# Two attention blocks whose value projection is computed by tokens and ahead of attention

## The chip, the cores and the metric

The program runs on one core of a Trainium2 chip. The metric is the device time of one execution in microseconds; lower is better. The engines named below are TensorE (PE in the profile), VectorE (DVE), ScalarE (ACT), GpSimd (POOL) and SyncE (SP, which here issues nearly all DMAs). Each runs its own instruction stream in order and waits on semaphores that the others raise.

## The reference

Two transformer stacks of two layers run one after the other on 512 tokens with 1024 features, all in float32. The change touches the input projections of the first stack's two attention mixers:

```python
# layer 0, hybrid mixer: n is the RMS-normed input (512 x 1024)
proj = n @ w_in                      # 3 x 512 (dilated) + 3 x 512 (forgetting) + 8 forget gates
qa, ka, va, qb, kb, vb, fb = split(proj)
oa = dilated_attention(rope(qa) * s, rope(ka), va)
ob = forgetting_attention(qb * s, kb, vb, cumsum(log_sigmoid(fb + b_f)))
h  = h + concat(oa, ob) @ w_out
# layer 1, differential mixer
q, k, v = split(n @ w_qkv)           # 3 x 1024; rope on all of q and k
o  = (softmax(q1 k1^T) - lam * softmax(q2 k2^T)) @ v       # 8 heads, v 128 wide
h  = h + subln(o) @ w_out
```

A gated feed-forward block follows each mixer; the second stack (gated linear attention, latent attention, convolutions) is untouched.

## The kernel before

**Weights and precision.** All large products go by "weight tiles": 128 output features by 1024 input features (512 KB), 25 of them in the hybrid projection (8 q, 8 k, 8 v, one for the forget gate) and 24 in the differential one. SP loads a tile into `raw`, ACT rounds it to `whi` (`split_hi`, L656), POOL subtracts to get `wlo` (`split_lo`, L566; from tile 14 of the differential projection on DVE does it, `split_lo_dve`, L573), and PE multiplies in `gemm` (L685 to L687): for each of 8 slices of 128 input features three matmuls, `whi` with `n_hi`, `whi` with `n_lo`, `wlo` with `n_hi`, 24 matmuls of 512 columns a tile, into one of two `G` banks. There are two slots for tiles, so the split of tile n+2 waits for the product of tile n.

**The norm's factor.** `n_hi` and `n_lo` hold the input times the gain, not yet divided by its root mean square. `norm_sum` on PE adds the squares (two float32 matmuls into bank S), ACT makes `rstd` from the sum by Ln and Exp (`rms_scale_act`, L775 and L776), and DVE multiplies each product by `rstd` as it takes it out of PSUM (`take_scaled`, L672). In the hybrid block the sum stands behind half of the second tile, in the differential block behind half of the first.

**Tiles, ahead of attention and in it.** q and k tiles leave the product with features on partitions, as attention wants them. A value tile must have tokens on partitions, so DVE takes it to `vst`, PE transposes it in four 128x128 blocks into bank X (`transpose_pe`, L1300), and DVE copies it to `v` (`keep_v_dve`, L1315). Four tiles (q0, k0, q1, k1) come ahead of attention; the others follow in its steps, 6 of the 8 slices of a tile in each step, in the order v0 q2 k2 v1 q3 k3 and so on. After a q or k tile SP turns its halves by four DMAs (L530) and DVE ropes it in three operations (L1322 to L1324), in the hybrid block for heads 0 to 3 only.

**Attention steps.** Each block has 32 units (8 heads or pairs of heads by 4 blocks of queries, the longest first: 512, 384, 256 and 128 keys), and 37 steps. In step s PE makes the scores of unit s, with every fourth step the value products (L1839 and L2071) of a head that is through, then the transposes of the probabilities of unit s-2, then the projection's slices of this step, and in the differential block every fourth step the head's norm sum (L2092). DVE takes the scores out with mask and maximum (L1968, L2200), scales the probabilities of the unit before, and then does what the tiles ask; ACT does the exponentials, copies the transposes to `pt`, and splits the next tile. The scores of unit s+1 wait until both halves of unit s are taken out of bank S (`masked`). When the input tiles are used up, the eight tiles of the first half of the output projection follow at one in a step (12 matmuls each), and two more begin in the last steps.

## Time and profile before

| | |
|---|---|
| device time, three runs | 2508.21, 2508.33, 2510.48 us (median 2508.33) |
| span of the profiled execution | 2506.5 us |
| PE busy | 2457.9 us (98%) |
| DVE, ACT, POOL busy | 1567.8 (63%), 1038.5 (41%), 975.0 (39%) |
| mean granted TensorE clock | 0.998 |
| hybrid attention, first to last scores | 34.59 to 225.48 us |
| differential attention, first to last scores | 649.61 to 836.87 us |

For the profiled execution the profile gives the span from first to last instruction; the device times come from runs of their own, 1.8 us above it at the median. Busy shares are averages over all stages; what a change in a stage is worth is read from that stage's waits. A matmul record of 0.39 us is the passage of one matmul; in a stream of them one starts every 0.227 us.

### The profile page before, as it was taken

Reading aid. Unit: us, or ns where it says so; the run is one execution under the profiler, and the core shown is the slowest. Engines: PE = TensorE matmul, PEld = TensorE weight load, DVE = VectorE, ACT = ScalarE, POOL = GpSimd, SP = SyncE. Lnnn points to the kernel's source line nnn. Section 1 sums busy time; section 2 is a strip of 40 time slices with the busy share of each in tenths; the row PEclk is TensorE's granted clock in tenths of the full one; section 3 lists DMA queues with packets and bytes.
Section 4 is the critical chain, followed back from the end, with each engine's and each line's share of the span. In section 5 each row is a group of like instructions: output and inputs, shape, how many; then the busy total and the mean of one; then the engine's idle time right before and its main releaser. Section 6 shows DMA issues by size and latency. Waiting matters only on the chain.

```text
span 2506.5 us, 33281 instructions
## 1 busy us (share of the span) xinstructions
PE 2457.9 (98%) x11238; PEld 1900.1 (76%) x11238; DVE 1567.8 (63%) x2255; ACT 1038.5 (41%) x1574; POOL 975.0 (39%) x421
## 2 busy tenths in 40 slices
PE   9999999999999999999999999999999999999998
PEld 6777788888777688888777467888877746788886
DVE  7654663777677766177778657515557875751555
ACT  5444552332344554123463654313336365431333
POOL 2232444444310045444455034444455504443443
PEclk9999999999999999999999999999999999999999
DMA  5222323232322233223222022323322202222232
GB/s 178 88 82 66 97 92 105 92 103 94 101 86 79 64 101 101 91 92 105 80 88 71 14 70 82 104 88 101 105 80 88 76 13 72 84 102 91 92 105 80
DMA packets 66510, 219.59 MB, mean 88 GB/s; under 512 B 8552, under 2 KB 8808, under 8 KB 66288
## 3 DMA queue, kind: packets, MB, share of 16 engines
q1 hardware_dynamic: 64384, 214.79, 26.2%
q10 hardware_dynamic: 2032, 3.56, 0.4%
q8 instruction: 58, 0.95, 0.2%
q14 instruction: 36, 0.29, 0.0%
HBM read 209.91 MB, written 2.11 MB: 85 GB/s over the span
## 4 chain that ended last, share of the span: by engine, by line
PE 86%; DVE 6%; ACT 3%; issue 3%; POOL 1%; DMA 0%; SPq 0%; DVEq 0%; POOLq 0%; ACTq 0%
PE bank_G L685 25%; PE bank_G L687 25%; PE bank_G L686 25%; PE bank_X L2435 1%; PE bank_S L1825 1%; PE bank_X L1853 1%; PE bank_O L2071 1%; PE bank_O L1839 1%; PE bank_S L2060 1%; PE bank_S L1612 1%; PE bank_S L2339 1%; PE bank_O L1622 1%; PE bank_O L2536 1%; PE bank_X L2083 0%; PE bank_X L2524 0%
## 5 line engine op out<-in xcount | busy, mean ns | idle before, releaser
L566 POOL TENSOR_TENSOR wlo<-raw,whi 128x1024 fp32r<-128x1024 f32 (+2 forms) x361 | 884.4, 2451 | 1478.7 <-ACT whi L656 1423.4
L685 PE MATMUL bank_G<-n_hi,whi 128*128 128x512 f32 x2216 | 881.8, 398 | 7.9 <-POOL wlo L566 3.2
L687 PE MATMUL bank_G<-n_hi,wlo 128*128 128x512 f32 x2216 | 864.1, 390 | 0.0
L686 PE MATMUL bank_G<-n_lo,whi 128*128 128x512 f32 x2216 | 863.3, 390 | 0.0
L656 ACT ACTIVATE whi<-raw 128x1024 fp32r<-128x1024 f32 (+2 forms) x389 | 404.3, 1041 | 676.0 <-PE bank_G L687 675.4
L685 PEld LDWEIGHTS bank_G<-n_hi,whi 128*128 128x128 f32 x2216 | 416.5, 188 | 110.3 <-issue 13.2
L687 PEld LDWEIGHTS bank_G<-n_hi,wlo 128*128 128x128 f32 x2216 | 416.1, 188 | 88.2
L686 PEld LDWEIGHTS bank_G<-n_lo,whi 128*128 128x128 f32 x2216 | 416.6, 188 | 86.8 <-issue 4.3
L685 PE MATMUL bank_G<-a_hi,whi 128*128 128x512 f32 x704 | 275.2, 391 | 0.0
L686 PE MATMUL bank_G<-a_lo,whi 128*128 128x512 f32 x704 | 274.1, 389 | 0.0
L687 PE MATMUL bank_G<-a_hi,wlo 128*128 128x512 f32 x704 | 274.0, 389 | 0.0
L2001 DVE TENSOR_TENSOR h<-h,bank_G 128x512 f32<-128x512 f32 x88 | 60.3, 686 | 158.2 <-PE bank_G L687 158.2
L686 PEld LDWEIGHTS bank_G<-a_lo,whi 128*128 128x128 f32 x704 | 132.2, 188 | 28.2 <-issue 0.7
L685 PEld LDWEIGHTS bank_G<-a_hi,whi 128*128 128x128 f32 x704 | 132.2, 188 | 28.0 <-issue 0.7
L687 PEld LDWEIGHTS bank_G<-a_hi,wlo 128*128 128x128 f32 x704 | 132.2, 188 | 27.3
L1145 ACT ACTIVATE a_hi<-prod 128x512 f32 (+1 forms) x88 | 55.7, 633 | 232.7 <-DVE prod L1209 232.7
L1209 DVE TENSOR_TENSOR prod<-silu,up 128x512 f32<-128x512 f32 x44 | 86.8, 1973 | 64.3 <-ACT silu L1152 64.3
L1211 DVE TENSOR_TENSOR a_lo<-prod,a_hi 128x512 f32 (+1 forms) x88 | 64.0, 727 | 80.1 <-ACT a_hi L1145 80.1
L1094 DVE SCALAR_TENSOR_TENSOR h<-h,bank_G 128x512 f32 x24 | 16.5, 687 | 144.8 <-PE bank_G L687 144.8
L1202 DVE TENSOR_SCALAR conv_up<-bank_G,vec 128x512 f32<-128x512 f32 x42 | 31.5, 750 | 110.3 <-PE bank_G L687 110.3
L2883 DVE SCALAR_TENSOR_TENSOR bank_O<-cpad,vec,bank_O 128x512 f32<-128x512 f32 x116 | 78.3, 748 | 3.8 <-DVE decayed L2390 2.8
L1195 DVE SCALAR_TENSOR_TENSOR conv<-gate,vec,conv 128x512 f32<-128x512 f32 x46 | 68.6, 1492 | 7.1 <-DVE conv L1194 7.0
(358 smaller groups left out, 2859.7 us busy)
## 6 DMA issues: line engine op xcount, KB each, us to landing
raw<-in_w_mix_in SPq DMA_DIRECT2D x40, 512.0 KB, 3.3
raw<-in_w_hyb_in SPq DMA_DIRECT2D x25, 512.0 KB, 3.3
raw<-in_w_diff_in SPq DMA_DIRECT2D x24, 512.0 KB, 3.3
raw<-in_w_up0a SPq DMA_DIRECT2D x22, 512.0 KB, 3.3
raw<-in_w_up0b SPq DMA_DIRECT2D x22, 512.0 KB, 3.2
raw<-in_w_up1a SPq DMA_DIRECT2D x22, 512.0 KB, 3.2
raw<-in_w_up1b SPq DMA_DIRECT2D x22, 512.0 KB, 3.2
raw<-in_w_up2a SPq DMA_DIRECT2D x22, 512.0 KB, 3.3
```

Source lines behind the costliest of these rows:

```text
L566: pool.tensor_tensor(b.wlo[:, g.slot, w], b.raw[:, g.slot, w], b.whi[:, g.slot, w], ALU.subtract).then_inc(b.lo_ready, 1)
L656: act.activation(b.whi[:, g.slot, w], b.raw[:, g.slot, w], ACT.Copy).then_inc(b.hi_ready, 1)
L685: pe.matmul(out, b.whi[:, g.slot, w], hi[:, hi_at + k, :], start=(k == 0), stop=False)
L686: pe.matmul(out, b.whi[:, g.slot, w], lo[:, lo_at + k, :], start=False, stop=False)
L687: mm = pe.matmul(out, b.wlo[:, g.slot, w], hi[:, hi_at + k, :], start=False, stop=(k == pieces - 1))
L1145: act.activation(b.a_hi[:, j, :], b.prod[:, :], ACT.Copy).then_inc(b.act_hi, 1)
L1195: return dve.scalar_tensor_tensor(dst[:, :], src[:, s + 2:s + 2 + T], v_(b, w, 2 * FC + c), dst[:, :], ALU.mult, ALU.add)
L1202: link(dve.tensor_scalar(dst[:, :], src, v_(b, w, FC + c), None, ALU.mult))
L1209: dve.tensor_tensor(b.prod[:, :], b.silu[:, :], up, ALU.mult).then_inc(b.prod_done, 1)
L1211: dve.tensor_tensor(b.a_lo[:, at, :].rearrange("p a t -> p (a t)"), b.prod[:, :], b.a_hi[:, at, :].rearrange("p a t -> p (a t)"), ALU.subt ...
L2001: dve.tensor_tensor(h, h, b.G[:, g.slot, :], ALU.add).then_inc(b.evacuated, 1)
L2883: dve.scalar_tensor_tensor(b.O[:, j, :], b.cpad[:, j, bass.ds(i + (first + 1), T)], v_(b, f"cfm_dw{l}", 2 * i + (2 * first + 2 + j)), b.O[ ...
```

## The change

Both projections are rearranged in the same way.

- **Value tiles.** A value tile is now 256 input features by 512 output features (the host rearranges the weights). The normed input is the stationary side and the weights move: for each slice of 128 input features and each of the four blocks of 128 tokens, three matmuls of 512 columns. Four tiles fill four PSUM banks with half of the value matrix, tokens on partitions; eight tiles make all of it. A tile still has 24 matmuls. The first half goes to X0, X1, O0, O1, the second to S1, S0, X0, X1.
- **The factor.** It is now one number per partition. `norm_sum` stands behind the second value tile in both blocks; behind the third, four small matmuls turn `rstd` into a column per token block in G, DVE copies it (`keep_column_dve`), and ACT takes the eight banks out with that scale (`keep_values_act`). Taking to `vst`, the transposes and the copies to `v` are gone.
- **Order.** The eight value tiles come first, then q0, k0, q1, k1: twelve tiles ahead of attention. The others (and the forget gate, thirteenth in the hybrid block) follow in attention, 4 slices, half a tile, in each step, q and k in turn. SP's turning DMAs in the opening of the program go with the q and k tiles to their later place.

```diff
--- before.py
+++ after.py
 POST_HYB = 0
-POST_DIFF = POST_HYB + 8 + 64
-POST_NORM = POST_DIFF + 8 + 32
+POST_DIFF = POST_HYB + 64
+POST_NORM = POST_DIFF + 32
 POST_MIX = POST_NORM + 8
...
-    gemm(pe, b, Index(a.g0), b.n_hi, b.n_lo, KD, lambda k: pe.wait_ge(b.nlo_ready, k + 1))
-    gemm(pe, b, Index(a.g0 + 1), b.n_hi, b.n_lo, KD, None, range(KD // 2))
-    pe.wait_ge(b.square_in, 16)
-    norm_sum(pe, b, 0)
-    gemm(pe, b, Index(a.g0 + 1), b.n_hi, b.n_lo, KD, None, range(KD // 2, KD))
+    value_tiles_pe(pe, b, a, 0, 0)
...
-    first_gemms_n(pe, b, ATT_DIFF.g0, 24, 2)
+    value_tiles_pe(pe, b, ATT_DIFF, 24, 2)
     inputs_start_pe(pe, b, ATT_DIFF)
 
 
 def hyb_in_act(act, b):
     for n in range(1, ATT_HYB.lead):
+        if n in VALUE_ENDS:
+            keep_values_act(act, b, ATT_HYB, VALUE_ENDS.index(n))
         split_hi(act, b, Index(ATT_HYB.g0 + n + 2))
 
 
 def diff_in_act(act, b):
     for n in range(ATT_DIFF.lead):
+        if n in VALUE_ENDS:
+            keep_values_act(act, b, ATT_DIFF, VALUE_ENDS.index(n))
         split_hi(act, b, Index(ATT_DIFF.g0 + n + 2))
...
-def input_follow_pe(pe, b, a, n):
-
-    kind, o = a.tiles[n]
-    if kind == "v":
-        transpose_pe(pe, b, Index(a.g0 + n), Index(a.in_posts[n]), b.vst[:, o % 2, :])
+VALUE_TILES, VALUE_ENDS = 8, (3, 7)
+VALUE_COLUMNS = 4 * P
+def value_bank(b, group, j):
+    return ((b.X, 0), (b.X, 1), (b.O, 0), (b.O, 1))[j] if group == 0 else ((b.S, 1), (b.S, 0), (b.X, 0), (b.X, 1))[j]
+def value_tile_pe(pe, b, a, n, nlo):
+    g, (group, t) = Index(a.g0 + n), divmod(n, 4)
+    pe.wait_ge(b.lo_ready, g.n + 1)
+    for s in range(2):
+        k, w = 2 * t + s, slice(s * VALUE_COLUMNS, (s + 1) * VALUE_COLUMNS)
+        pe.wait_ge(b.nlo_ready, nlo + k + 1)
+        for j in range(NB):
+            x, slot = value_bank(b, group, j)
+            if group == 1 and k == 0 and j >= 2:
+                pe.wait_ge(b.v_kept, VALUE_TILES * a.n + j - 1)
+            out, rows = x[:, slot, :], slice(j * P, (j + 1) * P)
+            pe.matmul(out, b.n_hi[:, k, rows], b.whi[:, g.slot, w], start=(k == 0), stop=False)
+            pe.matmul(out, b.n_lo[:, k, rows], b.whi[:, g.slot, w], start=False, stop=False)
+            mm = pe.matmul(out, b.n_hi[:, k, rows], b.wlo[:, g.slot, w], start=False, stop=(k == KD - 1))
+            if k == KD - 1 and j < NB - 1:
+                mm.then_inc(b.v_done, 1)
+    mm.then_inc(b.gemm_done, 1)
+def value_tiles_pe(pe, b, a, nlo, q):
+    for n in range(VALUE_TILES):
+        value_tile_pe(pe, b, a, n, nlo)
+        if n == SUM_BEHIND[a.n]:
+            pe.wait_ge(b.square_in, 16)
+            norm_sum(pe, b, q)
+        if n == 2:
+            pe.wait_ge(b.rstd_ready, q + 1)
+            pe.wait_ge(b.evacuated, a.g0)
+            for j in range(NB):
+                mm = pe.matmul(b.G[:, 1, 2 * j:2 * j + 2], b.rstd[:, j * P:(j + 1) * P], b.k["ident"][:, 0:2],
+                               start=True, stop=True)
+            mm.then_inc(b.column_done, 1)
+SUM_BEHIND = (1, 1)
+def keep_values_act(act, b, a, group):
+    act.wait_ge(b.column_kept, a.n + 1)
+    for j in range(NB):
+        x, slot = value_bank(b, group, j)
+        if j < NB - 1:
+            act.wait_ge(b.v_done, (NB - 1) * (2 * a.n + group) + j + 1)
+        else:
+            act.wait_ge(b.gemm_done, a.g0 + VALUE_ENDS[group] + 1)
+        act.activation(b.v[:, j, group * VALUE_COLUMNS:(group + 1) * VALUE_COLUMNS], x[:, slot, :], ACT.Copy,
+                       scale=b.small[:, 8 + j:9 + j]).then_inc(b.v_kept, 1)
+def keep_column_dve(dve, b, a):
+    dve.wait_ge(b.column_done, a.n + 1)
+    dve.tensor_copy(b.small[:, 8:8 + NB], b.G[:, 1, 0:2 * NB].rearrange("p (j a) -> p j a", a=2)[:, :, 0]).then_inc(b.column_kept, 1)
+    dve.wait_ge(b.column_kept, a.n + 1)
+    dve.sem_inc(b.evacuated, VALUE_TILES)
...
-    for n in range(1, a.lead):
-        if n > 1:
-            input_gemm_pe(pe, b, a, n)
+    for n in range(VALUE_TILES, a.lead):
+        input_gemm_pe(pe, b, a, n)
+    pe.wait_ge(b.v_kept, VALUE_TILES * (a.n + 1))
+
+
+def inputs_start_dve(dve, b, link, a):
+    keep_column_dve(dve, b, a)
+    for n in range(VALUE_TILES, a.lead):
+        input_take_dve(dve, b, a, n)
         if followed(a, n - 1):
-            input_follow_pe(pe, b, a, n - 1)
-
-
-def inputs_start_dve(dve, b, link, a):
-    for n in range(a.lead):
-        input_take_dve(dve, b, a, n)
-        if n and followed(a, n - 1):
...
 def in_turn():
 
-    tiles = [(x, o) for o in range(2) for x in "qk"]
-    for o in range(8):
-        tiles.append(("v", o))
-        if o + 2 < 8:
-            tiles += [("q", o + 2), ("k", o + 2)]
-    return tiles
-
-
-HYB_TILES = in_turn()[:4] + [("f", 0)] + in_turn()[4:]
+    return [("v", o) for o in range(8)] + [(x, o) for o in range(8) for x in "qk"]
+
+
+HYB_TILES = in_turn()[:12] + [("f", 0)] + in_turn()[12:]
 DIFF_TILES = in_turn()
 
...
-        plan_inputs(self, HYB_TILES, 4, 6, 4)
+        plan_inputs(self, HYB_TILES, 12, 4, 4)
...
-        plan_inputs(self, DIFF_TILES, 4, 6, 8)
+        plan_inputs(self, DIFF_TILES, 12, 4, 8)
...
-    v_kept_pe(pe, b, a, o)
...
-    v_kept_pe(pe, b, a, h)
...
+def value_weight_tiles(w):
+
+    k, m = w.shape
+    tiles = w.reshape(k // (2 * P), 2, P, m // VALUE_COLUMNS, VALUE_COLUMNS).transpose(3, 0, 2, 1, 4)
+    return np.ascontiguousarray(tiles).reshape(VALUE_TILES, P, k)
```

What stands in a row changes most in three places. The first is PE at the start of the differential block, around the norm's sum. In the rows, L762 to L770 are that sum, L685 to L687 the three matmuls of a slice before, L1428 to L1430 the same for a value tile. Before:

```order
L687 MATMUL bank_G<-n_hi,wlo 128x512
L767 MATMUL bank_S<-acc,const 128x512 [waits acc_ready]
L769 MATMUL bank_S<-sq,const 128x512 [waits last_ready]
L685 MATMUL bank_G<-n_hi,whi 128x512 [waits nlo_ready]
L686 MATMUL bank_G<-n_lo,whi 128x512
L687 MATMUL bank_G<-n_hi,wlo 128x512
```

and after the change:

```order
L1428 MATMUL bank_O<-whi,n_hi 128x512
L1429 MATMUL bank_O<-whi,n_lo 128x512
L1430 MATMUL bank_O<-wlo,n_hi 128x512
L768 MATMUL bank_S<-acc,const 128x512 [waits acc_ready,square_in]
L770 MATMUL bank_S<-sq,const 128x512 [waits last_ready]
L1428 MATMUL bank_X<-whi,n_hi 128x512 [waits nlo_ready,lo_ready]
L1429 MATMUL bank_X<-whi,n_lo 128x512
L1430 MATMUL bank_X<-wlo,n_hi 128x512
```

Before, the sum stands within the first tile; now it stands behind the second, and the matmul behind it is the first of the third tile, which waits for that tile's `wlo` (`lo_ready`).

The second place is ACT at the same point: L656 (L657 after the change) is `split_hi`, L775 and L776 (L776 and L777) are the Ln and Exp that make `rstd`, L1464 takes value banks out. Before:

```order
L656 ACTIVATE whi<-raw 128x1024 [waits gemm_done,loaded0]
L784 ACTIVATE n_hi<-h,vec 128x512 [waits evacuated] x2
L780 ACT_TABLE_LOAD
L775 ACTIVATE rstd<-bank_S,small 128x512 [waits sum_done]
L776 ACTIVATE rstd<-rstd 128x512 [waits act_order]
L656 ACTIVATE whi<-raw 128x1024 [waits gemm_done,loaded1]
L656 ACTIVATE whi<-raw 128x1024 [waits gemm_done,loaded0]
```

and after:

```order
L657 ACTIVATE whi<-raw 128x1024 [waits gemm_done,loaded0]
L785 ACTIVATE n_hi<-h,vec 128x512 [waits evacuated] x2
L781 ACT_TABLE_LOAD
L776 ACTIVATE rstd<-bank_S,small 128x512 [waits sum_done]
L777 ACTIVATE rstd<-rstd 128x512 [waits act_order]
L657 ACTIVATE whi<-raw 128x1024 [waits gemm_done,loaded1]
L657 ACTIVATE whi<-raw 128x1024 [waits gemm_done,loaded0]
L657 ACTIVATE whi<-raw 128x1024 [waits gemm_done,loaded1]
L1464 ACTIVATE v<-bank_X,small 128x512 [waits v_done,column_kept]
L1464 ACTIVATE v<-bank_X,small 128x512 [waits v_done]
L1464 ACTIVATE v<-bank_O,small 128x512 [waits v_done]
L1464 ACTIVATE v<-bank_O,small 128x512 [waits gemm_done]
L657 ACTIVATE whi<-raw 128x1024 [waits gemm_done,loaded0]
```

The split behind `rstd` is that of the third tile in both; what is new in the row are the four copies of value banks, ahead of the split of the sixth tile.

The third place is PE at the end of differential attention, from the scores of the last unit on: L2060 are scores, L2083 the transposes of probabilities, L2092 a head's norm sum, L2071 the last head's value products (17 lines lower after the change: L2078, L2100, L2109, L2088). Before:

```order
L2060 MATMUL bank_S<-qk 128x128 [waits masked]
L2060 MATMUL bank_S<-qk 128x128
L2083 MATMUL bank_X<-const,probs 128x128 [waits x_free1,scaled]
L2083 MATMUL bank_X<-const,probs 128x128 x2
L685 MATMUL bank_G<-heads,whi 128x512 [waits evacuated,lo_ready]
L686 MATMUL bank_G<-heads,whi 128x512
L687 MATMUL bank_G<-heads,wlo 128x512
L685 MATMUL bank_G<-heads,whi 128x512
```

and after:

```order
L2078 MATMUL bank_S<-qk 128x128 [waits masked]
L2078 MATMUL bank_S<-qk 128x128
L2100 MATMUL bank_X<-const,probs 128x128 [waits x_free1,scaled]
L2100 MATMUL bank_X<-const,probs 128x128 x2
L2109 MATMUL bank_X<-mixed,const 128x512 [waits x_free0,sub_sq]
L2100 MATMUL bank_X<-const,probs 128x128 [waits x_free1,scaled]
L2100 MATMUL bank_X<-const,probs 128x128
L2100 MATMUL bank_X<-const,probs 128x128 [waits x_free0,scaled]
L2088 MATMUL bank_O<-pt,v 128x512 [waits sub_tmp,x_free0]
L2088 MATMUL bank_O<-pt,v 128x384
```

Before, a tile of the output projection (12 matmuls, from the row with `lo_ready` on) stands behind each of the last three groups of transposes; after the change none stands between the last scores and the last value products.

## Rows read from the trace of the kernel before

**Rows 1.** Page, part 4: the chain that ended last, by engine.

```profile
PE 86%; DVE 6%; ACT 3%; issue 3%; POOL 1%; DMA 0%; SPq 0%; DVEq 0%; POOLq 0%; ACTq 0%
```

**Rows 2.** Timeline, PE: start us, length us, line, operands, count.

```profile
56.76 0.60 PE L1300 MATMUL bank_X<-const,vst 128*128 128x128 f32 x4
57.29 1.13 PE L1825 MATMUL bank_S<-qk 64*128 64x512 f32 x4
```

**Rows 3.** Timeline, start of the hybrid block; in brackets idle time before, and releaser.

```profile
18.73 1.10 PE L762 MATMUL bank_S<-acc,const 128*128 128x512 f32 x2 [1.37 <-DVEq L3022]
19.07 2.37 POOL L566 TENSOR_TENSOR wlo<-raw,whi 128x1024 fp32r<-128x1024 f32 x1 [18.62 <-DVEq L3022]
20.12 0.79 PE L685 MATMUL bank_G<-n_hi,whi 128*128 128x512 f32 x1
```

**Rows 4.** Timeline, start of the differential block.

```profile
628.71 1.02 PE L767 MATMUL bank_S<-acc,const 128*128 128x512 f32 x2
629.68 2.38 POOL L566 TENSOR_TENSOR wlo<-raw,whi 128x1024 fp32r<-128x1024 f32 x1 [7.31 <-DVE n_lo L789]
630.63 0.69 ACT L775 ACTIVATE rstd<-bank_S,small 128x512 f32<-128x512 f32 x1 [0.79 <-PE bank_S L769]
631.35 0.63 ACT L776 ACTIVATE rstd<-rstd 128x512 f32<-128x512 f32 x1
633.46 1.06 ACT L656 ACTIVATE whi<-raw 128x1024 fp32r<-128x1024 f32 x1 [1.48 <-PE bank_G L687]
634.67 2.39 POOL L566 TENSOR_TENSOR wlo<-raw,whi 128x1024 fp32r<-128x1024 f32 x1 [2.61 <-ACT whi L656]
638.84 0.69 DVE L672 SCALAR_TENSOR_TENSOR qk<-bank_G,rstd 128x512 f32<-128x512 f32 x1 [4.67 <-PE bank_G L687]
```

**Rows 5.** Timeline, PE: one set of value products in either latent attention.

```profile
1425.56 5.35 PE L1622 MATMUL bank_O<-pt,mx 128*64 128x512 f32 x16 [2.15 <-ACT pt L1657]
2051.10 3.65 PE L1622 MATMUL bank_O<-pt,mx 128*64 128x512 f32 x16 [2.15 <-ACT pt L1657]
```

**Rows 6.** Windows: stretch, its length, busy us (count) by engine, clock, DMA.

```profile
1254.05:1260.90 6.85, 6.85 (x31) 5.63 (x30) 5.06 (x10) 6.68 (x12) 1.29 (x1) 1.00 0.08 16
1425.56:1429.20 3.64, 3.64 (x10) 1.15 (x12) 2.55 (x8) 1.72 (x4) 0.00 (x0) 0.54 0.00 0
```

**Rows 7.** Timeline, PE: the small matmul for lambda.

```profile
263.74 0.38 PE L2028 MATMUL bank_S<-lamp,const 64*128 64x2 f32 x2
```

**Rows 8.** Timeline: first steps of attention, hybrid block (first row) and differential.

```profile
40.56 0.92 PE L1825 MATMUL bank_S<-qk 64*128 64x384 f32 x4 [0.49 <-DVE nmax L1968]
649.61 1.13 PE L2060 MATMUL bank_S<-qk 64*128 64x512 f32 x4
651.64 2.78 DVE L1324 TENSOR_TENSOR qk<-qk,sq 128x512 f32<-128x512 f32 x1
655.70 0.92 PE L2060 MATMUL bank_S<-qk 64*128 64x384 f32 x4 [0.64 <-DVE nmax L2200]
```

**Rows 9.** Windows: four steps of differential attention, columns as in rows 6.

```profile
722.79:747.45 24.66, 24.66 (x114) 17.61 (x113) 18.11 (x44) 11.82 (x28) 0.00 (x0) 1.00 0.29 86
```

**Rows 10.** Waits of PE in all of differential attention: total us, times, longest.

```profile
PE bank_S L2060 <- DVE nmax L2200: 1.8, 3, 0.8
```

**Rows 11.** Timeline: a tile's split on DVE and its turning DMAs; landing time.

```profile
740.58 2.41 SPq L530 DMA_DIRECT2D sq<-qk  x4
742.27 1.22 DVE L573 TENSOR_TENSOR wlo<-raw,whi 128x1024 fp32r<-128x1024 f32 x1
...
DMA to landing us min/median/max: 1.9/2.0/2.7
```

**Rows 12.** Timeline: end of differential attention.

```profile
836.87 0.49 PE L2060 MATMUL bank_S<-qk 64*128 64x128 f32 x4
840.52 0.70 PE L2092 MATMUL bank_X<-mixed,const 128*128 128x512 f32 x1
...
847.35 2.32 PE L2071 MATMUL bank_O<-pt,v 128*128 128x512 f32 x8
```

More of the change, by code:

```diff
@@ L1423, in input_take_dve @@
     g = Index(a.g0 + n)
[L1424 to L1426 removed]
+    if kind == "f":
         take_scaled(dve, b, g, b.ntmp[:, 0, :])
@@ L1460, in inputs_pe @@
         input_gemm_pe(pe, b, a, n, part)
-    for n in follows(a, step):
-        input_follow_pe(pe, b, a, n)
 def inputs_act(act, b, a, step):
@@ L1523, in followed @@
     kind, o = a.tiles[n]
-    return kind == "v" or (kind in "qk" and o < a.roped)
+    return kind in "qk" and o < a.roped
 def follows(a, step):
     return [n for n in a.follows.get(step, ()) if followed(a, n)]
-def count_posts(a, post, order):
-    order = [x for x in order if x[0] != "in" or a.tiles[x[1]][0] == "v"]
-    assert len(set(order)) == len(order) and all(kind != "v" for kind, _ in a.tiles[:a.lead - 1])
-    a.in_posts = {n: post + order.index(("in", n)) for n, (kind, _) in enumerate(a.tiles) if kind == "v"}
-    return order
 class Attention:
@@ L1724, in __init__ @@
         self.g0 = FIRST["hyb_in"]
-        plan_inputs(self, HYB_TILES, 4, 6, 4)
-        order = []
-        for step in range(self.steps):
-            if 0 <= step - self.lag < self.units:
-                order += [("att", step - self.lag, x) for x in range(2)]
-            order += [("in", n) for n in follows(self, step)]
-        order = count_posts(self, post, order)
-        self.posts = [[post + order.index(("att", u, x)) for x in range(2)] for u in range(self.units)]
+        plan_inputs(self, HYB_TILES, 12, 4, 4)
+        self.posts = [[post + 2 * u + x for x in range(2)] for u in range(self.units)]
     def unit(self, u):
@@ L1775, in __init__ @@
                 order.append(("att", step - self.lag))
-            order += [("in", n) for n in follows(self, step)]
             if self.normed(step) is not None:
                 order.append(("norm", self.normed(step)))
-        order = count_posts(self, post, order)
         self.posts = [post + order.index(("att", u)) for u in range(self.units)]
```

32 lines of the change are left out of this document (13 added, 19 removed).

## The prediction, written before the changed kernel had run

> **What bounds the kernel.** I read the page's chain of waits first, then the waits of PE, the windows of the two attention blocks, and the timeline at the five places the change touches. PE carries 86% of the chain [rows 1] and streams matmuls nearly all the time. So two things count: instructions that PE no longer has, and PE idle time that appears or goes. Work on VectorE, ScalarE, GpSimd and the DMAs counts where PE waits for it. Inside differential attention PE waits for score takes only three times, 1.8 us in all [rows 10]; VectorE is busy 18.11 of 24.66 us in four steady steps [rows 9].
>
> **The change part by part.** The number of large matmuls is the same: 24 a tile at 0.227 us each (31 in 6.85 us [rows 6] is slightly less than that because one is cut by the window), 5.45 us a tile wherever it stands. Moving eight tiles out of the steps costs or gains nothing by itself.
>
> *Transposes of values.* Four of them hold PE from 56.76 to 57.29, when the scores start [rows 2]: 0.53 us. There are 16 sets, none waited for by PE. Gain 8.5 us.
>
> *Start of the hybrid block.* PE idled 1.37 us before the norm's sum, waiting for the squares [rows 3]. The sum now stands 12 matmuls (2.7 us) later: PE comes to it at 18.73 - 1.37 + 2.73 = 20.1, when the squares are there, and, with 1.75 us for the sum (18.73 to about 20.5, by its neighbour at 20.12 [rows 3]), to the third tile at 21.8. That tile's `wlo` ends at 19.07 + 2.37 = 21.44. The fourth tile's split stands behind `rstd`, but has a whole tile to be done in. Gain 1.4 us (1.0 to 1.4).
>
> *Start of the differential block.* ScalarE's row has the split of the third tile behind the Ln and Exp of `rstd`, which wait for the sum. Before, the sum started at 628.71, the Exp ended at 631.98, and the split waited only for the first tile's product at 633.4 [rows 4]. Now the sum stands behind the second tile. Before, two tiles and the sum ended at 638.84 [rows 4]; two tiles take 10.9 us and the sum 1.8, so the first began at 626.15. Now the first ends at 631.6, the second waits for its `wlo` until 629.68 + 2.38 = 632.06 and ends at 637.55. From the sum's first matmul to the end of the Exp was 631.98 - 628.71 = 3.27 us, so `rstd` is there at 640.9. Then the split, 1.21 us to the start of the subtraction (633.46 to 634.67) and 2.39 for that [rows 4]: 644.5, and the third tile starts at 644.6 where it started at 638.84. Loss 5.8 us (5.2 to 6.3), of which about 5.2 in one piece of idle PE. Nothing stands in PE's row that could fill it. The split of the fourth tile follows at once, so the loss is paid once.
>
> *The clock after it.* One idle stretch of 2.15 us was followed by 16 matmuls in 5.35 us, the other, equally long, by the same 16 in 3.65 us [rows 5]; in the first the granted clock was 0.54, near the lower level of 1.2 GHz for nearly the whole stretch [rows 6]. So such a stretch cost 1.7 us in one of two cases. The stall above is more than twice as long: I take one such cost, 1.7 us (0 to 3.4, since the end of the block idles too).
>
> *The column.* Four float32 matmuls of two columns a block, each in two passes. The nearest row, one of this kind with 64 rows, took 0.38 us from first start to end [rows 7]; four in a row overlap, so 0.2 to 0.4 each with the change of mode. I take 1.3 us a block (0.4 to 1.8), 2.6 in all. `rstd` is there by then. ScalarE's copies of value banks come ahead of a split at two places, 0.7 us late after overlap, against a slack of 5.45 - 1.06 - 2.4 = 2.0 us: nothing.
>
> *First step of attention.* Here VectorE is still roping: its last operation took 2.78 us, because GpSimd subtracted beside it, and the second scores started 6.09 us after the first, with 0.64 us of PE idle [rows 8]. That chain (take, ropes, two score takes) is unchanged, while PE has 6 matmuls (1.36 us) less in the step. Loss 1.4 us; the hybrid block had 0.49 us of such a wait [rows 8] and comes to 1.2. Together 2.6 us (1.0 to 3.5).
>
> *The steady steps, differential block.* Four steps took 24.66 us with three tiles of input in them [rows 9]. Now they hold two: 24.66 - 5.45 - 0.53 = 18.7 us of PE. VectorE loses a take and a copy of 0.69 each and a split of 1.22 [rows 11]: 18.11 - 2.6 = 15.5 us busy, 83%. It has room on average, but is in order and waits itself: a rope now comes one step after its tile, and its turned halves land 2.41 + 2.0 us after the take [rows 11], where the step before left some 3.6; the split waits for ScalarE, which has the exponentials first; and the head's norm sum waits for a square that stands behind them. Following the four steps with these durations, I find about 0.4 us more than 18.7, 2 us over five groups. Against it, GpSimd's last subtraction now falls in the first step, and with it goes the wait behind a rope slowed by it, 0.8 us [rows 10]. I take 1 us net (-0.8 to 10). In the hybrid block ropes end after head 3 and I find 0.5 us, as much as fewer switches between the two kinds of matmul give back: nothing.
>
> *The end of attention.* The output tiles start three steps earlier in the differential block (step 23, not 26), so none stands behind the last scores. Before, 836.87 to 847.35, 10.5 us, held three of them, 8.6 us (12 matmuls and a change of mode, 2.86 each), and 1.9 us of PE's own work [rows 12]. The chain beside it is: residual and subtraction on VectorE, then takes, exponential, copy, square: the norm sum started 3.65 us after the scores [rows 12]. Then its Ln and Exp stand on ScalarE before the copy of the last transposes. By hand the value products then start 6.8 us after the scores. Loss 6.8 - 1.9 = 4.9 us (3 to 6). In the hybrid block only the copy of the last transposes lies open: 1.0 us (0.3 to 1.5).
>
> Sum: -8.5 - 1.4 + 5.8 + 1.7 + 2.6 + 2.6 + 1.0 + 4.9 + 1.0 = +9.7 us, on the profiled span of 2506.5. The median of the runs is 1.8 us above that span, and I carry that along: 2508.3 + 9.7 = 2518.0 us. The value products, output products and feed-forward blocks are as before.
>
> *A rule against the change.* Value tiles go through four PSUM banks, three matmuls to each. The nearest stretch alternates between two banks every three matmuls and shows 31 matmuls in 6.85 us at a clock of 1.00 [rows 6], so the sum charges nothing. The Trainium skill (TensorE: Matmul & The Clock Gate, section "A second HAM failure mode: psum-queue depth-cycling") says that a kernel which cycled through banks idled so often in between that its clock swung between the two levels. By that rule the 16 value tiles could run at half speed; the trace so far speaks against it.
>
> **Rivals.** (1) *Relief wins, no loss of time.* VectorE and ScalarE have 16 takes, copies and transposes fewer, no tile is late, the steady waits vanish (-0.8), the clock does not fall, the column costs 0.8, first steps 1.0, both ends 3.3: -8.5 - 1.4 + 5.8 - 0.8 + 0.8 + 1.0 + 3.3 = +0.2, 2508.5 us. For it: 83% busy and only 1.8 us of waits. Against: the three lost covers can be read from the rows. It comes out not slower once the ends and first steps cost less than 4 us together; for clearly faster the stall would have to be shorter by 4 us as well. (2) *VectorE becomes the bound in differential attention*: if each group of four steps takes 20.7 us, not 18.7 + 0.4, five groups add 8 more: 2526 us. For it: order and waits as above. Against: the slack of 3.2 us a group. (3) *Bank cycling halves the clock in the value tiles*: 16 x 5.45 = 87 us more, 2605 us; the two-bank stretch speaks against it.
>
> **Chances.** Forecast (2512 to 2523) 0.60; rival 1 0.20, of which 0.07 clearly faster; rival 2 0.14; rival 3 0.02; others 0.04. What this kernel's measurement can tell from no change is 0.2%, 5 us. Slower 0.75, within it 0.18, faster 0.07. Adding the bounds gives -0.4 to +24.8 us, 2508 to 2533; both ends at once are unlikely above, and clearly faster has its 0.07 below, so the range is 2507 to 2526 us; the forecast's own range is 2512 to 2523.
>
> **What would show it.** Right: PE idle of some 5 us before the third value tile of the differential block, released by GpSimd's subtraction, with a clock at half behind it; no idle before the hybrid sum; two idle stretches of some 2 us before the second scores; two of 1 to 3 us before the last norm sum but one and the last value products; groups of four steps at 19 to 19.5 us. Wrong: no idle before the third tile; groups over 20 us; value matmuls more than 0.23 us apart; or a result below 2507.

## The result and the profile after

| | before | after |
|---|---|---|
| device time, median (runs) | 2509.27 us (4) | 2531.16 us (4) |
| span of the profiled execution | 2506.5 us | 2529.7 us |
| mean granted TensorE clock | 0.998 | 0.994 |

The changed kernel is slower: ratio 1.0089, 95% interval 1.0078 to 1.0101, 22 us where 9.7 were forecast, and outside the range. The chain of the page, part 4, answers to [rows 1]; PE's share has fallen, that of DVE has risen:

```profile
PE 84%; DVE 7%; ACT 3%; issue 3%; POOL 1%; DMA 1%; SPq 0%; POOLq 0%; ACTq 0%; DVEq 0%
```

The timeline of PE at the norm's sum of the hybrid block, answering to [rows 3]. No idle time stands before it any more:

```profile
20.89 0.39 PE L1430 MATMUL bank_O<-wlo,n_hi 128*128 128x512 f32 x1
21.11 1.02 PE L763 MATMUL bank_S<-acc,const 128*128 128x512 f32 x2
```

The timeline at the start of the differential block, answering to [rows 4]: the split of the third tile (`whi`) stands behind the two activations for `rstd`, GpSimd's subtraction behind it, and PE idles 4.89 us. The last row is the column, eight passes; between the matmuls on either side it takes 0.8 us:

```profile
645.81 0.69 ACT L776 ACTIVATE rstd<-bank_S,small 128x512 f32<-128x512 f32 x1 [9.78 <-PE bank_S L770]
646.53 0.63 ACT L777 ACTIVATE rstd<-rstd 128x512 f32<-128x512 f32 x1
647.07 1.99 ACT L657 ACTIVATE whi<-raw 128x1024 fp32r<-128x1024 f32 x2
648.26 4.67 POOL L567 TENSOR_TENSOR wlo<-raw,whi 128x1024 fp32r<-128x1024 f32 x2 [10.00 <-ACT whi L657]
650.66 0.80 PE L1428 MATMUL bank_X<-whi,n_hi 128*128 128x512 f32 x1 [4.89 <-POOL wlo L567]
...
658.76 0.95 PE L1447 MATMUL bank_G<-const,rstd 128*128 128x2 f32 x8
```

The timeline of the first steps of the hybrid block, answering to [rows 8]:

```profile
84.41 0.92 PE L1844 MATMUL bank_S<-qk 64*128 64x384 f32 x4 [1.99 <-DVE nmax L1986]
91.13 0.42 DVE L1378 TENSOR_SCALAR ntmp<-ntmp 8x512 f32<-8x512 f32 x1
91.24 2.57 POOL L567 TENSOR_TENSOR wlo<-raw,whi 128x1024 fp32r<-128x1024 f32 x1 [8.66 <-ACT whi L657]
91.47 2.88 DVE L1379 SCALAR_TENSOR_TENSOR mixed<-ntmp 8x512 f32<-8x512 f32 x1
95.48 0.49 PE L1844 MATMUL bank_S<-qk 64*128 64x128 f32 x4 [1.22 <-DVE nmax L1986]
97.37 1.00 PE L1871 MATMUL bank_X<-const,probs 128*128 128x128 f32 x6 [1.40 <-ACT pt L1934]
...
102.44 2.40 POOL L567 TENSOR_TENSOR wlo<-raw,whi 128x1024 fp32r<-128x1024 f32 x1 [8.63 <-ACT whi L657]
102.85 2.08 DVE L1993 TENSOR_SCALAR probs<-probs,rden 128x128 f32<-128x128 f32 x1
106.80 0.57 PE L1871 MATMUL bank_X<-const,probs 128*128 128x128 f32 x2 [0.29 <-ACT pt L1934]
```

The forget gate's last operation on VectorE, 8 rows wide, lasts 2.88 us and ends just behind GpSimd's subtraction beside it; then the fourth scores and a set of transposes come late. In the steady steps the same happens to a scaling of probabilities (2.08 us; the same operation takes 0.28 alone), and PE waits 0.29 us behind it in each group of four steps.

The timeline at the end of differential attention, answering to [rows 12]: the head's norm sum, the last transposes and the value products each wait.

```profile
860.03 0.49 PE L2078 MATMUL bank_S<-qk 64*128 64x128 f32 x4
863.68 1.52 PE L2109 MATMUL bank_X<-mixed,const 128*128 128x512 f32 x2 [2.68 <-ACT mixed L2160]
866.78 0.45 PE L2100 MATMUL bank_X<-const,probs 128*128 128x128 f32 x1 [1.14 <-ACT mean L2174]
867.59 4.15 PE L2088 MATMUL bank_O<-pt,v 128*128 128x512 f32 x8 [0.37 <-ACT pt L2152]
```

Windows of the changed kernel (columns as in [rows 6]; the fourth answers to [rows 9], but lies in the hybrid block). The first begins where an idle stretch of PE ends, the second 1.3 us and the third 0.1 us before that, and the clock is near its lower level of 1.2 GHz (0.50 in the column behind GpSimd's would be that level throughout) for much or all of each:

```profile
84.41:89.79 5.38, 5.38 (x17) 3.61 (x17) 3.65 (x10) 2.30 (x8) 0.00 (x0) 0.68 0.17 66
649.40:656.20 6.80, 5.54 (x13) 4.38 (x14) 0.00 (x0) 0.00 (x0) 3.54 (x2) 0.51 0.50 154
863.60:870.40 6.80, 5.21 (x9) 2.35 (x10) 1.58 (x3) 2.50 (x6) 0.00 (x0) 0.55 0.00 2
101.06:120.78 19.72, 19.38 (x102) 13.00 (x101) 14.96 (x36) 10.54 (x27) 4.76 (x2) 1.00 0.27 81
```

**The account.** From the starts of scores in both traces, with 5.45 us taken off for each tile and 0.53 for each set of transposes that stands elsewhere or is gone:

| stretch | forecast | measured |
|---|---|---|
| transposes | -8.5 | -8.5 |
| hybrid block up to its scores, column included | -0.1 | +0.1 |
| first four steps, hybrid | +1.2 | +6.0 |
| next twenty steps, hybrid | 0 | +3.8 |
| hybrid end | +1.0 | +0.7 |
| differential block up to its scores (stall, clock, column) | +8.8 | +9.2 |
| first four steps, differential | +1.4 | +1.5 |
| next sixteen steps, differential | +1.0 | +0.8 |
| differential end | +4.9 | +8.5 |
| later (half clock at one place more) | 0 | +1.1 |
| sum, on the span | +9.7 | +23.2 |

Three rows carry most of the error (12.2 of 13.5 us): the first and the steady steps of the hybrid block, and the differential end.

### The profile page after: what moved, and what is told of

The parts are those of the page before. It is cut to its first block, busy times and chain, and to the rows that moved or that the text cites. A ratio compares the mean times of both kernels' runs of the same rounds, so it can differ in the third digit from the quotient of the medians.

```text
span 2529.7 us, 33159 instructions
## 1 busy us (share of the span) xinstructions
PE 2464.9 (97%) x11190; PEld 1898.6 (75%) x11190; DVE 1538.0 (61%) x2225; ACT 1048.9 (41%) x1590; POOL 973.5 (38%) x421
## 4 chain that ended last, share of the span: by engine, by line
PE 84%; DVE 7%; ACT 3%; issue 3%; POOL 1%; DMA 1%; SPq 0%; POOLq 0%; ACTq 0%; DVEq 0%
PE bank_G L686 24%; PE bank_G L688 24%; PE bank_G L687 24%; PE bank_X L2452 1%; POOL wlo L567 1%; PE bank_S L2356 1%; PE bank_O L2088 1%; PE bank_O L1649 1%; PE bank_S L1639 1%; PE bank_X L1871 1%; PE bank_S L1844 1%; PE bank_X L1428 1%; PE bank_O L2553 1%; PE bank_O L1857 1%; PE bank_X L1430 1%
## 5 line engine op out<-in xcount | busy, mean ns | idle before, releaser
L686 PE MATMUL bank_G<-n_hi,whi 128*128 128x512 f32 x2088 | 830.6, 398 | 6.8 <-POOL wlo L567 3.2
L688 PE MATMUL bank_G<-n_hi,wlo 128*128 128x512 f32 x2088 | 814.1, 390 | 0.0
L687 PE MATMUL bank_G<-n_lo,whi 128*128 128x512 f32 x2088 | 813.6, 390 | 0.0
L657 ACT ACTIVATE whi<-raw 128x1024 fp32r<-128x1024 f32 (+2 forms) x389 | 404.3, 1040 | 698.4 <-PE bank_G L688 659.3
L686 PEld LDWEIGHTS bank_G<-n_hi,whi 128*128 128x128 f32 x2088 | 392.7, 188 | 102.5 <-issue 12.7
L688 PEld LDWEIGHTS bank_G<-n_hi,wlo 128*128 128x128 f32 x2088 | 392.3, 188 | 83.8
L687 PEld LDWEIGHTS bank_G<-n_lo,whi 128*128 128x128 f32 x2088 | 392.7, 188 | 81.6 <-issue 3.8
L687 PE MATMUL bank_G<-a_lo,whi 128*128 128x512 f32 x704 | 273.9, 389 | 0.0
L687 PEld LDWEIGHTS bank_G<-a_lo,whi 128*128 128x128 f32 x704 | 132.1, 188 | 28.1 <-issue 0.7
L673 DVE SCALAR_TENSOR_TENSOR qk<-bank_G,rstd 128x512 f32<-128x512 f32 x32 | 22.1, 690 | 103.4 <-PE bank_G L688 103.3
```

What stands on the lines that cost most here:

```text
L657: act.activation(b.whi[:, g.slot, w], b.raw[:, g.slot, w], ACT.Copy).then_inc(b.hi_ready, 1)
L686: pe.matmul(out, b.whi[:, g.slot, w], hi[:, hi_at + k, :], start=(k == 0), stop=False)
L687: pe.matmul(out, b.whi[:, g.slot, w], lo[:, lo_at + k, :], start=False, stop=False)
L688: mm = pe.matmul(out, b.wlo[:, g.slot, w], hi[:, hi_at + k, :], start=False, stop=(k == pieces - 1))
```

## The experiments

Each median is of 4 to 11 runs and is compared with 2531.16 us of the changed kernel; ratios are to the kernel before, with 95% intervals of 0.0009 to 0.0016 on either side. So a difference of two kernels is known to some 3 to 4 us, and where it is less (-2.1, -2.7, -2.9 and +1.5 us below) the verdict rests on the trace.

### The order without the tokens

The kernel before with `in_turn` giving the values first, twelve tiles ahead and four slices in a step:

```
+    return [("v", o) for o in range(8)] + [(x, o) for o in range(8) for x in "qk"]
-        plan_inputs(self, HYB_TILES, 4, 6, 4)
+        plan_inputs(self, HYB_TILES, 12, 4, 4)
```

> The kernel before, with the change's order of tiles alone: values first, twelve tiles ahead of attention, four slices of a tile in a step, but values by features with TensorE's transposes, as before. Theory: of the 22 us that the whole change costs, the order costs all and more (first steps, shorter steps in which VectorE, GpSimd and ScalarE are late, the ends of attention), since by tokens it saved 8.5 us of transposes and 1.4 at the start, and lost about 8.5 us by the norm's place and 2.6 by the column: 2525 to 2533, 16 to 24 us over before. Rival, the value tiles by tokens carry the loss (their stall, clock and late copies) and the order is nearly free: 2509 to 2516.

Measured: 2529.99 us, ratio 1.0085 (1.0071 to 1.0098), as expected. The order alone makes nearly the whole loss, with the same waits: 2.00 us at the second scores, 1.22 and 1.40 behind the gate, 0.29 in each group, 2.67 at the last but one norm sum, and half clock behind the first, behind its like in the differential block, and behind the last. The tokens' part comes out at about zero net: 8.5 us of transposes gained, and about as much lost where the norm's sum was put.

### The stall at the start of the differential block

```
-SUM_BEHIND = (1, 1)
+SUM_BEHIND = (1, 0)
```

> The changed kernel, with the sum of squares of the differential block's norm put behind the first value tile instead of the second. Theory: ScalarE's split of the third value tile stands behind the norm's two activations, so the third tile's weights are late (TensorE idle for 4.9 us), and the clock then drops to half for 6.8 us of dense work (3.4 us lost). With the sum ahead of the second tile the split is issued 7.3 us of TensorE work earlier: both go, the time falls by 7 to 9 us against the changed kernel. Rival, the late weights are late by the transfer or by GpSimd and not by ScalarE's order: the idle time stays within 2 us of 4.9 and the time falls by less than 3. Rival, the clock drop has another cause than the idle stretch: the idle time goes, the half clock stays, minus 5 us.

Measured: 2523.25 us, 7.9 less, as expected. The timeline shows the split done early, and PE running from the second tile (bank O) into the third (bank X) without a gap:

```profile
639.37 1.04 ACT L657 ACTIVATE whi<-raw 128x1024 fp32r<-128x1024 f32 x1
640.58 2.39 POOL L567 TENSOR_TENSOR wlo<-raw,whi 128x1024 fp32r<-128x1024 f32 x1 [3.74 <-ACT whi L657]
643.18 0.39 PE L1430 MATMUL bank_O<-wlo,n_hi 128*128 128x512 f32 x1
643.41 0.39 PE L1428 MATMUL bank_X<-whi,n_hi 128*128 128x512 f32 x1
```

To part the idle time from the clock, the next kernel keeps the stall and fills it:

```
             norm_sum(pe, b, q)
+            if a.n == 1:
+                pe.wait_ge(b.evacuated, a.g0)
+                for _ in range(5):
+                    pe.matmul(b.G[:, 0, :], b.k["ones"], b.const[:, SQUARE:SQUARE + T], start=True, stop=True)
```

> The changed kernel, with five matmuls of 512 columns in float32 (0.85 us each, read by nothing) behind the differential block's sum of squares, in the stretch where TensorE stood idle for 4.9 us. Nothing waits for them but TensorE, and they end at about 650.0, before the third tile's weights are there (650.66). Theory: half the clock follows from idle time, so that with TensorE kept busy the 6.8 us at 1.2 GHz behind the stretch go back to full speed, and the time falls by about 3.4 us though the third tile starts as late as before. Rival: the drop comes from the form of the value tiles themselves (four accumulating banks taken in turn, moving weights): the fill changes nothing, within 1 us, or costs what it overruns.

Measured: 2529.11 us, 2.1 less. Its timeline, with the column behind the third tile (L1451 here), and a window of 6.8 us from the third tile on, then the same window of the changed kernel:

```profile
646.26 4.46 PE L1446 MATMUL bank_G<-const 128*128 128x512 f32 x10
651.31 0.50 PE L1428 MATMUL bank_X<-whi,n_hi 128*128 128x512 f32 x1 [0.60 <-POOL wlo L567]
...
656.89 0.95 PE L1451 MATMUL bank_G<-const,rstd 128*128 128x2 f32 x8
...
651.31:658.11 6.80, 6.80 (x34) 5.78 (x35) 0.16 (x1) 0.97 (x1) 2.30 (x1) 1.00 0.41 154
```

```profile
650.66:657.46 6.80, 6.80 (x19) 5.37 (x20) 0.00 (x0) 0.00 (x0) 2.27 (x1) 0.60 0.50 154
```

The third tile comes as late as before (at 651.31, against 650.66), but the clock stays at 1.00. Its 24 matmuls end at the column 5.6 us after they begin, where the changed kernel needs 8.1 (650.66 to 658.76). The counts of the windows, 34 and 19, exaggerate this: 8 of the 34 are the column's short passes. From the third tile's start to the first scores it took 55.6 us, not 58.1: the drop cost 2.5 us, less than the 3.4 expected, since a part of the 6.8 us at half clock lay in the idle time. The bank cycling of the value tiles costs nothing: over four banks one matmul starts every 0.23 us (24 in 5.6 us), as elsewhere.

### The first steps

```
-    a.parts, a.ends, a.follows = {}, {}, {0: [lead - 1]}
+    a.parts, a.ends, a.follows = {}, {}, {0: [lead - 2], 1: [lead - 1]}
```

> The changed kernel in which VectorE does the rotary embedding of the last two tiles ahead of attention (in both blocks) inside the first attention steps, behind the takes of the scores, instead of ahead of them. Theory: the second scores of each block wait for VectorE (1.99 us in the hybrid, 2.00 us in the differential block) because its queue still holds the ropes; with those behind, the waits go, and the half clock behind the one in the hybrid block (3.4 us of stretch, 1.4 us lost) goes too: minus 4 to 5.5 us. Rival, the ropes only change place, and the same waits come one or two steps later, where the ropes now stand (the third or fourth scores, or the transposes that need ScalarE's copies): within 1.5 us of no change.

Measured: 2528.45 us, 2.7 less: between the two. Both waits of 2 us went, but in the hybrid block the delay came back two steps later, larger, in the timeline at the fourth scores (and the clock fell to half behind it); in the differential block 1.00 us came back:

```profile
86.23 4.34 POOL L567 TENSOR_TENSOR wlo<-raw,whi 128x1024 fp32r<-128x1024 f32 x1 [5.49 <-ACT whi L657]
86.46 0.67 DVE L1379 SCALAR_TENSOR_TENSOR mixed<-ntmp 8x512 f32<-8x512 f32 x1
87.06 0.67 DVE L1316 TENSOR_TENSOR qk<-qk,const 128x512 f32<-128x512 f32 x1
87.66 0.67 DVE L1317 TENSOR_TENSOR sq<-sq,const 128x512 f32<-128x512 f32 x1
88.37 2.74 DVE L1318 TENSOR_TENSOR qk<-qk,sq 128x512 f32<-128x512 f32 x1
92.25 0.80 PE L1844 MATMUL bank_S<-qk 64*128 64x128 f32 x4 [2.99 <-DVE nmax L1986]
```

The other way, rotating each tile ahead of the next take, before attention:

```
+        if followed(a, n - 1):
+            input_follow_dve(dve, b, link, a, n - 1)
         input_take_dve(dve, b, a, n)
```

> The changed kernel, in which VectorE, ahead of attention, rotates a tile before it takes the next one out of its bank (and not after), in both blocks. So the rotation of the last but one tile is done while TensorE still multiplies the last one, and VectorE comes to the first scores right after one take. Theory: the waits of 1.99 and 2.00 us at the second scores go in both blocks, and with them the half clock behind the one of the hybrid block (1.4 us): minus 4 to 5.5 us. Rival, as with the last rotations put into the steps: the delay returns two or three steps later, because these steps are paced by VectorE and by GpSimd's subtractions that it waits out: within 1.5 us of no change.

Measured: 2537.83 us, 6.7 more: both expectations missed. The timeline shows why. The rotation waits for the turned halves, and the last take, now queued behind it, and the first scores with it:

```profile
81.84 0.73 DVE L1316 TENSOR_TENSOR qk<-qk,const 128x512 f32<-128x512 f32 x1 [4.01 <-DMA sq<-qk]
83.82 0.68 DVE L673 SCALAR_TENSOR_TENSOR qk<-bank_G,rstd 128x512 f32<-128x512 f32 x1
84.42 0.68 DVE L1986 CUSTOM_DVE_ANT_0 probs<-bank_S,const 128x512 f32<-128x512 f32 x1
85.78 0.92 PE L1844 MATMUL bank_S<-qk 64*128 64x384 f32 x4 [3.44 <-DVE nmax L1986]
```

The forget gate's tile ahead of attention:

```
-HYB_TILES = in_turn()[:12] + [("f", 0)] + in_turn()[12:]
+HYB_TILES = in_turn()[:8] + [("f", 0)] + in_turn()[8:]
```

> The changed kernel, with the forget gate's tile of the hybrid block computed ahead of attention, right behind the value tiles (thirteen tiles ahead), and its ScalarE and VectorE steps there too. Theory: the waits of 1.22 us (fourth scores) and 1.40 us (transposes) come from VectorE's 8-row operation of the gate, which takes 2.88 us beside GpSimd's subtraction, and from ScalarE's two activations behind it: both waits go, minus 2 to 3 us; the input tiles end two steps earlier, which costs up to 1 us at the end. The wait of 1.99 us at the second scores stays. Rival, the waits belong to the steps' length and not to the gate: they stay within 1 us.

Measured: 2532.66 us, 1.5 more, no gain where 2 to 3 us were expected. What is left of the gate's work in the steps, the running sum, met GpSimd in turn: it took 3.43 us where it takes 1.21 alone, and the fourth scores waited 1.48 us (1.22 before this edit), the transposes behind them 0.71 (1.40).

```profile
95.51 2.39 POOL L567 TENSOR_TENSOR wlo<-raw,whi 128x1024 fp32r<-128x1024 f32 x1 [8.56 <-ACT whi L657]
95.55 3.43 DVE L1393 TENSOR_TENSOR_SCAN negc<-small,mixed 8x512 f32<-8x512 f32 x1
100.09 0.49 PE L1846 MATMUL bank_S<-qk 64*128 64x128 f32 x4 [1.48 <-DVE nmax L1986]
```

This points to GpSimd as the cause and the gate as its victim; the next pair tests it.

### GpSimd's subtractions

VectorE makes the low parts of the hybrid block's tiles from the fifteenth on:

```
+        for n in a.ends.get(step, ()):
+            if 14 <= n + 2 < len(a.tiles):
...
+                split_lo_dve(dve, b, Index(a.g0 + n + 2))
```

> The changed kernel, with the low parts of the hybrid block's weight tiles made by VectorE from the fifteenth tile on, as the differential block already does it, and no longer by GpSimd. Theory: in the hybrid block's shorter steps VectorE's operations between two SBUF tiles wait out GpSimd's 2.4 us subtraction (a scaling of 0.28 us takes 2.08, a maximum of 0.67 takes 2.88), and ScalarE's copies and TensorE's transposes wait behind (0.29 us visible in every four steps, some 0.75 in all). With GpSimd out of these steps and 1.23 us more on VectorE for each tile, the steady steps lose their 0.75 us per four and the forget gate's waits (1.22 and 1.40 us) shrink: minus 3 to 6 us. Rival: VectorE's own load is what is short; 1.23 us more in every second step costs as much as the wait saves: within 1.5 us, or slower.

Measured: 2524.76 us, 6.4 less, just beyond what was expected. The gate's last operation, which took 2.88 us, again takes 0.67, the fourth scores no longer wait, and none of the five waits of 0.29 us is left. The timeline shows that operation (L1383 here), then the windows: four steady steps, which took 19.72 us, and the step behind the wait of 1.99 us, which is the same but was followed by no drop of the clock in this execution (3.79 us, not 5.38):

```profile
88.79 0.67 DVE L1383 SCALAR_TENSOR_TENSOR mixed<-ntmp 8x512 f32<-8x512 f32 x1
...
96.62:116.02 19.40, 19.26 (x102) 13.21 (x101) 13.71 (x38) 10.30 (x27) 0.00 (x0) 1.00 0.27 82
83.31:87.10 3.79, 3.79 (x16) 2.47 (x16) 3.65 (x10) 2.06 (x7) 0.00 (x0) 1.00 0.21 79
```

VectorE's busy time fell from 14.96 to 13.71 us although it does more: operations that wait out GpSimd count as busy. In this trace, against that of the changed kernel, the first four steps are 3.3 us shorter (1.6 of them clock) and the next twenty 2.4 us. So without the clock, which fell or did not by chance, the edit's places account for 4.1 us; the medians' 6.4 us is known to some 3 to 4 us only and agrees with that. Of the 7.0 us by which these two stretches exceed the forecast without the clock (3.2 and 3.8), 2.9 us remain with GpSimd out (1.5 and 1.4), and no run parts them. The control is the same edit in the kernel before:

> The kernel before, with the low parts of the hybrid block's tiles made by VectorE from the fifteenth tile on. It says whether the 6.4 us that this edit gave the changed kernel are the change's own loss or were there before. Theory: in the kernel before, a step holds six slices of a tile, TensorE never waits in the hybrid block's steady steps (24.99 us busy of 24.99), so GpSimd's subtractions hurt nobody: within 1 us of the kernel before. Rival: the edit frees time in both, and the kernel before gains 3 us or more by it; then the prediction's step on the steady steps was right, and the gain has nothing to do with the change.

Measured: 2508.78 us, ratio 1.0002 (0.9993 to 1.0011), as expected. Four steps in its window, with the edit at work, still take 24.97 us, all of it PE. GpSimd's collisions were there before and cost nothing; the shorter steps laid them bare.

```profile
131.68:156.65 24.97, 24.97 (x130) 17.98 (x129) 14.21 (x41) 11.49 (x29) 0.00 (x0) 1.00 0.26 85
```

### The end of differential attention

```
+        a.outs = {step: m for m, step in enumerate((23, 24, 25, 27, 29, 31, 32, 33))}
-        m = step - a.out_step
+        m = a.outs.get(step)
```

> The changed kernel, with the eight first output tiles of the differential block spread out to the end of attention: at steps 23, 24, 25, 27, 29, 31, 32 and 33 instead of 23 to 30, so that the last ones again stand beside the waits of the last steps, as in the kernel before (26 to 33). Theory: the loss of some 8.5 us between the sixth head and the end of the block is made of waits of the last steps that nothing covers any more (2.68, 1.14, 0.37 us at the last head's normalization) and of 6.8 us at half clock behind them (3.4 us): both go, and the steps left without a tile cost 1 to 3 us back: minus 3 to 6 us. Rival, the waits move into the steps without a tile, where VectorE sets the pace, and the clock falls there instead: within 1.5 us of no change.

Measured: 2528.29 us, 2.9 less, just short of what was expected. In its trace, which is of the fastest of its five runs (2524.72 us), the stretch from the 21st scores to the end of the block (800.18 to 890.93) is 90.8 us where the changed kernel had 94.8. The waits of 2.68, 1.14 and 0.37 us and the drop of the clock behind them are gone. But the timeline shows what the steps without a tile cost, and from just before its second row on the clock was at half for a shorter stretch (0.50 from 843.50 to 846.90), so the rival was right in part:

```profile
842.11 0.92 PE L2081 MATMUL bank_S<-qk 64*128 64x384 f32 x4 [1.30 <-DVE nmax L2220]
843.90 0.45 PE L2103 MATMUL bank_X<-const,probs 128*128 128x128 f32 x1 [0.87 <-ACT mean L2177]
...
855.29 1.02 PE L2112 MATMUL bank_X<-mixed,const 128*128 128x512 f32 x2
```

### Together

Four of the edits above in one kernel, and then the three that paid, then these with VectorE's splits:

> The changed kernel with four edits together: the sum of squares behind the first value tile in the differential block, the output tiles held back, rotations ahead of takes, the forget gate ahead of attention. If the losses are separate and each is what the theory says (8 + 4.5 + 4.5 + 2.5 us), the time is about 2512, within 3 us of the kernel before on either side. Rival, the clock and the pace of VectorE give some of it back: 2516 to 2522.

Measured: 2526.82 us. With what the four edits cost and gave alone (-7.9, -2.9, +6.7, +1.5) it should be 2528.6: they add, but two of them are losses, and both expectations (2512, 2516 to 2522) missed.

> The changed kernel with the three edits together that each measured below it: the sum of squares behind the first value tile (minus 7.9 us), the last rotations inside the first attention steps (minus 2.7), the output tiles held back (minus 2.9). If the losses are separate places of one program they add up: 2516 to 2519. Rival, they share the clock's drops, which then fall elsewhere: 2520 to 2524.

Measured: 2515.71 us, ratio 1.0027 (1.0017 to 1.0037); -7.9, -2.7 and -2.9 give 2517.7. The three add up.

> The kernel with three edits, and VectorE making the hybrid block's low parts from the fifteenth tile on, in GpSimd's place. Theory: the gain of that edit alone (3 to 6 us expected) comes on top: 2511 to 2515, which would leave the order's cost nearly undone. Rival: 2516 or more.

Measured: 2510.38 us, ratio 1.0007 (0.9998 to 1.0016), 20.8 less than the changed kernel, where the four edits alone sum to 19.9. The net loss is undone, and there it stops: not measurably faster than the kernel before. So the 8.5 us of transposes that the change saves are still lost elsewhere. Part of that is seen: the first four hybrid steps take 20.9 us, where 16.7 would be without any loss, the next twenty 1.4 us too long, and at the differential end waits of up to 1.30 us stand.

> As the kernel with three edits, and the input tiles handed out by five slices in each of the first eight steps (then four), the output tiles again to step 33. Theory: what is left in the first steps (VectorE late for the fourth scores by 3 us in the hybrid block) is for want of TensorE's work beside it; a fifth slice gives 0.68 us more per step, and the work that it takes from the later steps costs little there: minus 1 to 4 us against the kernel with three edits. Rival: the later steps then wait as much (steps of the last heads with no tile in them): no change within 1.5 us.

The main line of the edit, in `plan_inputs` (the output tiles of the differential block stand at other steps too, the last at 33):

```
-        step = at // slices
+        step = at // 5 if at < 40 else 8 + (at - 40) // 4
```

Measured: 2521.82 us, 6.1 more than with three edits, so both expectations missed. The fourth scores' wait fell from 3.00 to 0.98 us, but new waits stood in the following steps (0.87, 0.46 and 1.85 us) and at the ends of both blocks. Longer first steps only move the shortage.

> The changed kernel with the four edits that were run together, and the forget gate's tile and steps ahead of attention, with the hybrid block's first output tiles spread over steps 23 to 32. Theory: the 2.07 us at the fourth scores of the hybrid block and the half clock behind them (1.7 us) hang on VectorE's work for the gate: minus 2 to 4 us, 2506.5 to 2508.5, as fast as the kernel before or just faster. Rival: as with the gate's move alone, the wait stays (the fourth scores wait for VectorE's backlog of the second and third), and the steps without a tile at the end cost 1 to 2 us: 2510 to 2512.

Measured: 2512.67 us, ratio 1.0017 (1.0007 to 1.0026): the rival, but for 0.7 us. The fourth scores waited 2.33 us, not 2.07; whatever else delays VectorE in steps two and three was not tried apart.

## Why the prediction was wrong

**Right.** The transposes; the hybrid start; the stall, forecast at 5.2 us in one piece behind ScalarE's queue and measured at 4.89, shown by the sum's move; both second-score waits of some 2 us; the differential block's steady steps (+0.8 for +1.0); the waits at the differential end (8.5 less an estimated 2.6 for the clock, against 4.9); the hybrid end; no cost of the banks; the column, 1.6 us where 2.6 were taken.

**The step that failed first: "nothing" for the hybrid block's steady steps**, and with it "comes to 1.2" for its first ones. They were priced from PE's work and VectorE's durations in steps where PE never waited. But the durations of VectorE in [rows 8] already held the mechanism, 2.78 us for an operation of 0.69 beside GpSimd; I used it for that one rope and took it for gone elsewhere. It returned at the gate (2.6 us of waits) and in each group of four steps (0.29 us visible as a wait). Of the 3.8 us lost in twenty steady steps, taking GpSimd out gave 2.4 back, and of the 3.2 us in the first steps 1.7, in this kernel and none in the one before. The other 2.9 us lie in the same steps, and their cause stays open.

**The mis-sized term: the clock, 1.7 us.** I charged one drop. The trace has new ones at the hybrid first steps (1.6 us, by the same step with and without), behind the stall (2.5 us), at the differential end (some 2.6: 5.21 us busy at 0.55 in the window, and a little behind it), and at one place more in the latent attentions (about 1). That is some 7.7 us in place of 1.7. Only the first two are measured against a trace without the drop; the third is an estimate from its window. Each new wait of about 2 us was a possible drop, and I had named several such waits beside the stall.

Of the 13.5 us that the forecast fell short, the clock makes about 6 and the hybrid block's waits about 7 (3.2 in the first steps beyond the forecast ones, 3.8 in the steady ones); the rest is differences of 1 us or less that nearly cancel. Rival 2 fell (differential groups take 19.3 us in the mean, and only the first of the four, 20.15, is above 20, not 20.7 each), and rival 3 too. Rival 1's time of 2508.5 us is near what the repaired kernel does, but not by its mechanism: there the waits and drops were taken away by four edits. A part of the clock's share is chance: the drop in the hybrid first steps and the second one in the latent attentions stand in this trace, but not in all that have the same waits.

## What to carry to other kernels

When work is moved out of the steps of a loop, price the steps by the chain of the other engines, and read their durations as they are under collision: an operation that often takes four times its least duration will end the step as soon as the cover is gone. Charge a possible clock drop to each new idle stretch of some 2 us, and to two shorter ones close together, not only to the longest. What is computed ahead must bring its own order on the splitting engine: the norm's place, one constant, was worth 8 us.

## What the runs showed of the hardware

The drop of the clock behind an idle stretch is not certain. Over the changed kernel and the experiments that keep these places, the stretch of 4.9 us was followed by half clock in every trace that had it (6 of 6), and so was the group of waits that begins with 2.7 us (8 of 8), but the wait of 2.0 us before the second scores only in 6 of 14 cases (4 of 7 in the hybrid block, 2 of 7 in the differential one), with the same instructions around it in each block. It also came with two shorter waits close together: with those of 1.22 and 1.40 us at the gate in 2 traces of 5, and with those of 1.30 and 0.87 us in 3 of the 5 kernels that hold the output tiles back to steps 23 to 33. So two profiles of kernels like these differ by 1.6 us at one such place by chance.

VectorE and GpSimd excluded each other on SBUF tiles, in both directions. Beside GpSimd's 2.4 us subtraction a two-input operation or a scaling of VectorE, whether 8 or 128 rows high, ended only behind it; but in the kernel with the late rotations, where VectorE had a run of such operations (0.67 us each), it was the subtraction that took 4.34 us, and VectorE's next one 2.74. The Trainium skill has a rule for this (SBUF — State Buffer, section "Who interferes with whom"): whoever comes first holds the shared pair of ports for its whole instruction, and an operation of VectorE with two SBUF inputs or in a two-port mode wants it. The traces agree that the two exclude each other. Who goes first is less simple in the kernel with the late rotations: the subtraction's row begins at 86.23, but three operations of VectorE that followed each other without a gap (86.46, 87.06, 87.66) still passed in their usual 0.67 us, and only the one behind a gap of 0.04 us (88.37) waited. The traces add that such a collision has no fixed price: for the same eleven tiles some 4 us in the trace (6.4 between the medians) where steps were short, nothing where TensorE covered them.
